# Units of gelu and gates: their loads move from SyncE's DMA queue to ScalarE's

## The reference, cut to what matters

```python
def peer(h, wq, k1, k2, u, v):
    ...
    experts = e1 * N_KEYS + e2
    gates = jax.nn.softmax(best, axis=-1).astype(h.dtype)
    ...
    def one_block(args):
        xb, eb, gb = args
        a = jnp.einsum("td,thkd->thk", xb, u[eb])
        act = gb * jax.nn.gelu(a)
        return jnp.einsum("thk,thkd->td", act, v[eb])
```

## Time and profile before

| | |
|---|---|
| median of 3 runs | 3135.79 us (3130.93 to 3138.95) |
| the profiled execution | 3137.47 us |
| its span, first to last instruction | 3135.7 us |
| TensorE busy | 2998.2 us (96%) |
| VectorE busy | 2533.5 us (81%) |
| ScalarE busy | 1030.0 us (33%) |
| GpSimd busy | 839.7 us (27%) |
| moved by DMA | 893.82 MB, mean 285 GB/s |
| queue q1 (SP) | 111376 packets, 491.29 MB |
| queue q0 (POOL) | 46080 packets, 335.56 MB |
| queue q10 (ACT) | 24624 packets, 64.45 MB |

### The profile page before, as it was taken

The page is one execution under the profiler, slowest core; times in us unless marked ns, Lnnn a source line. Parts: engine busy times, 40 slices in busy tenths (PEclk is TensorE's granted clock), DMA queues, the critical chain, the costliest instruction groups (busy, mean ns, idle before and its releaser), DMA issues.

```text
span 3135.7 us, 41987 instructions
## 1 busy us (share of the span) xinstructions
PE 2998.2 (96%) x17373; PEld 2759.4 (88%) x17373; DVE 2533.5 (81%) x3098; ACT 1030.0 (33%) x1081; POOL 839.7 (27%) x380
## 2 busy tenths in 40 slices
PE   5799989989989999999999999989999999999999
PEld 3687765557778899999999999989999999999999
DVE  7986968756673589999988998854989899898985
ACT  4323243341122333333333333323333334333331
POOL 5600000000030013333123333421444444444440
PEclk8999989989999999999999999999999999999999
DMA  9722223347744468888778988987999999999994
GB/s 368 268 94 77 81 85 138 124 168 302 290 159 180 142 228 326 333 333 321 274 266 343 356 346 337 389 330 285 375 395 389 390 392 392 395 386 398 385 399 164
DMA packets 182257, 893.82 MB, mean 285 GB/s; under 512 B 15680, under 2 KB 77248, under 8 KB 85824
## 3 DMA queue, kind: packets, MB, share of 16 engines
q1 hardware_dynamic: 111376, 491.29, 42.4%
q0 software_dynamic: 46080, 335.56, 26.2%
q10 hardware_dynamic: 24624, 64.45, 5.3%
HBM read 836.71 MB, written 54.53 MB: 284 GB/s over the span
## 4 chain that ended last, share of the span: by engine, by line
PE 84%; DVE 10%; DMA 2%; ACT 2%; issue 1%; SPq 0%; ACTq 0%; DVEq 0%; PEldq 0%
PE bank L1909 10%; PE bank L1911 10%; PE bank L1910 10%; PE bank L1968 10%; PE bank L1969 10%; PE bank L1970 10%; PE bank L1606 3%; PE bank L1608 3%; PE bank L1607 3%; DVE ada_w L944 2%; PE bank L1944 2%; PE bank L1843 2%; PE bank L1844 2%; PE bank L1845 2%; DMA ada_w<-wada 1%
## 5 line engine op out<-in xcount | busy, mean ns | idle before, releaser
L475 POOL DMA_INDIRECT u_row<-u_rows,urow_i x128 | 285.6, 2231 | 823.7 <-DVE u_row L1374 559.0
L1909 PE MATMUL bank<-act_hi,w_hi 128*128 128x352 f32 x1376 | 447.7, 325 | 8.0 <-DVE low L906 8.0
L1910 PE MATMUL bank<-act_lo,w_hi 128*128 128x352 f32 x1376 | 445.0, 323 | 0.0
L1968 PE MATMUL bank<-wt_hi,w_hi 128*128 128x352 f32 x1360 | 439.5, 323 | 4.9 <-DVE w_lo L906 4.4
L1969 PE MATMUL bank<-wt_lo,w_hi 128*128 128x352 f32 x1360 | 438.4, 322 | 0.0
L1911 PE MATMUL bank<-act_hi,low 128*128 128x352 f32 x1024 | 332.1, 324 | 0.0
L1911 PE MATMUL bank<-act_hi,w_lo 128*128 128x352 f32 x1024 | 330.3, 323 | 0.0
L1970 PE MATMUL bank<-wt_hi,w_lo 128*128 128x352 f32 x1024 | 330.3, 323 | 0.0
L1970 PE MATMUL bank<-wt_hi,low 128*128 128x352 f32 x1024 | 329.3, 322 | 0.0
L486 POOL DMA_INDIRECT u_row<-v_rows,urow_i x96 | 232.2, 2418 | 271.3 <-DVE y_g L1521 249.5
L1374 DVE SCALAR_TENSOR_TENSOR u_row<-u_row,h2t 128x2048 f32<-128x2048 f32 x128 | 288.9, 2288 | 13.4 <-DMA u_row<-u_rows,urow_i 13.3
(11 more groups left out here) (340 smaller groups left out, 7234.3 us busy)
## 6 DMA issues: line engine op xcount, KB each, us to landing
ada_w<-wada SPq DMA_DIRECT2D x80, 1024.0 KB, 5.5
w_raw<-u SPq DMA_DIRECT2D x64, 1024.0 KB, 5.9
raw<-u SPq DMA_DIRECT2D x64, 1024.0 KB, 5.6
w_raw<-v SPq DMA_DIRECT2D x64, 1024.0 KB, 9.1
raw<-v SPq DMA_DIRECT2D x64, 1024.0 KB, 6.8
w_raw<-win SPq DMA_DIRECT2D x27, 1024.0 KB, 4.9
gelu_scratch<-gelu_s ACTq DMA_DIRECT2D x128, 176.0 KB, 8.4
gate_scratch<-g_chunk ACTq DMA_DIRECT2D x11, 2048.0 KB, 12.2
```

The lines of the kernel that those rows point to most:

```text
L475: pool.indirect_dma_start(u_row[n % 3][:], None, urow_d, bass.IndirectOffsetOnAxis(ap=col, axis=0)).then_inc(u_row_loaded[n % 3], 16)
L1909: pe.matmul(out, wh[:, k, :], HD(k), start=(k == 0), stop=False)
L1910: pe.matmul(out, wh[:, k, :], LD(k), start=False, stop=False)
L1968: pe.matmul(o, wh[:, 8 * e + d, :], th, start=begin is not None and e == 0, stop=False)
```

## The change

`load_unit` leaves SP's program, whose queue then holds loads of weights alone, and goes into ScalarE's. SP also loses its waits for stored gelu and gates. Unit 0 is issued in `gelu_job`'s loop behind u = 115, unit 1 behind u = 120, unit 2 behind u = 125, unit 3 behind the `hi_raw` of v job 5, and unit 4 + 4i + r//4 behind the `hi_raw` of v job 6 + 16i + r where r % 4 == 2. Besides, `weigh_hi(0)` moves from u = 119 to 118, `weigh_hi(1)` from 124 to 123, and `weigh_lo(1)` from n = 126 to 125.

```diff
@@ SyncE
-            def load_unit(n):
-
-                if n:
-                    sp.wait_ge(wtl_ready, n)
-                rows = slice(4 * n, 4 * n + 4)
-                sp.dma_start(wt[:], gelu_d[:, rows, :]).then_inc(wt_loaded, 16)
-                sp.dma_start(gate_l[:], gate_d[:, :, rows, :].rearrange("c p i t -> p c i t")).then_inc(wt_loaded, 16)
-
-            for g in range(2, NKEY - 6):
+            for g in range(2, NKEY + 128):
                 load_raw(g)
-            for s in range(2):
-                sp.wait_ge(g_stored[s], DMA_LEAD + 16 * ((N_CH + 1 - s) // 2))
-                sp.wait_ge(gelu_stored[s], DMA_LEAD + 16 * 6)
-                sp.wait_ge(hot_used[2 * s + 1], LEAD + N_HOTS // 2)
-            load_unit(0)
...
-            load_unit(2)
-            for q in range(2, 128):
-                load_raw(NKEY + q)
-                if q == 2:
-                    for s in range(2):
-                        sp.wait_ge(gelu_stored[s], DMA_LEAD + 16 * NKEY // 2)
-                if q == 8:
-                    load_unit(3)
-                elif q % 4 == 2 and 10 <= q < 122:
-                    load_unit(4 + (q - 10) // 4)
@@ ScalarE
+            def load_unit(n):
+
+                if n:
+                    act.wait_ge(wtl_ready, n)
+                rows = slice(4 * n, 4 * n + 4)
+                act.dma_start(wt[:], gelu_d[:, rows, :]).then_inc(wt_loaded, 16)
+                act.dma_start(gate_l[:], gate_d[:, :, rows, :].rearrange("c p i t -> p c i t")).then_inc(wt_loaded, 16)
+
...
-                if u == 119:
+                if u == HOT + N_HOTS + 2:
+                    for s in range(2):
+                        act.wait_ge(g_stored[s], DMA_LEAD + 16 * ((N_CH + 1 - s) // 2))
+                        act.wait_ge(gelu_stored[s], DMA_LEAD + 16 * 6)
+                    load_unit(0)
+                if u == 118:
                     weigh_hi(0)
-                if u == 124:
+                if u == 120:
+                    load_unit(1)
+                if u == 123:
                     weigh_hi(1)
+                if u == 125:
+                    load_unit(2)
...
             for u in range(2):
                 act.wait_ge(gelu_stored[u], DMA_LEAD + 64 * 16)
+            load_unit(3)
...
                     if r % 4 == 0:
                         weigh_hi(3 + 4 * i + r // 4)
+                    if r % 4 == 2:
+                        load_unit(4 + 4 * i + r // 4)
@@ VectorE
-                elif n == 126:
+                elif n == 125:
                     weigh_lo(1)
```

More of the change, by code:

```diff
@@ L401, in _ @@
                 load_raw(u)
-            def load_unit(n):
-                if n:
-                    sp.wait_ge(wtl_ready, n)
-                rows = slice(4 * n, 4 * n + 4)
-                sp.dma_start(wt[:], gelu_d[:, rows, :]).then_inc(wt_loaded, 16)
-                sp.dma_start(gate_l[:], gate_d[:, :, rows, :].rearrange("c p i t -> p c i t")).then_inc(wt_loaded, 16)
-            for g in range(2, NKEY - 6):
-                load_raw(g)
-            for s in range(2):
-                sp.wait_ge(g_stored[s], DMA_LEAD + 16 * ((N_CH + 1 - s) // 2))
-                sp.wait_ge(gelu_stored[s], DMA_LEAD + 16 * 6)
-                sp.wait_ge(hot_used[2 * s + 1], LEAD + N_HOTS // 2)
-            load_unit(0)
[L418 to L422, removed]
-            load_unit(2)
-            for q in range(2, 128):
-                load_raw(NKEY + q)
-                if q == 2:
-                    for s in range(2):
-                        sp.wait_ge(gelu_stored[s], DMA_LEAD + 16 * NKEY // 2)
-                if q == 8:
-                    load_unit(3)
-                elif q % 4 == 2 and 10 <= q < 122:
-                    load_unit(4 + (q - 10) // 4)
+            for g in range(2, NKEY + 128):
+                load_raw(g)
         @block.gpsimd
```

## The result

The changed kernel takes **3168.51 us** (median of 4 runs, 3165.52 to 3169.83), against 3137.37 us for the kernel before in its 4 runs (3130.93 to 3142.16): ratio 1.0099, 95% interval 1.0079 to 1.0120, some 31 us **slower**. 3124 us were forecast. The time lies inside the range, on the side that the third rival (the gates starve, 3176 us, 30%) had named. The profiled execution took 3167.52 us; its span is 3165.7 us, 30.0 more than before. 893.82 MB are moved, as before; q10 (ACT) now carries 74800 packets, q1 (SP) 61200.

The account below looks back on a forecast made before the run. TensorE was taken as the bound, losing 24.9 us in three stalls behind late gates. Terms -2.0 - 13.9 + 3 + 1 = -11.9 turn the profiled 3137.5 into 3125.6; the runs' median is 1.7 lower: 3124 us, range 3107 to 3178.

Parts of the forecast that it names:

- third rival: Gates of units 4 to 31 starve at `weigh`, 2 us lost per unit on average: 3176 us, slower, chance 30%.
- What bounds the kernel: TensorE is full from 2250 to 3000 us; its idle time after 1400 us lies between 2050 and 2200 us.
- the three stalls: TensorE stalls while VectorE waits for gates of units 0, 1 and 3: 11.0, 6.8 and 7.1 us, together 24.9.
- The queue: Busy queues take turns packet by packet: 1408 gate packets need 2.4 us alone, 31 beside one queue, 56 beside two.
- ScalarE's own time: Two load issues a unit on ScalarE, at most 1.7 us each unit, claimed hidden: 0.
- SP: SP loses its unit issues and 16.6 us of waiting, so weights come sooner to a never idle TensorE: 0.
- Unit 0: Its 11.0 us stall: gates issued some 13 us sooner but landing near the old time; 2.0 us gained.
- a second way: Unit 0: gelu 116's store stands behind the unit's loads and `gelu_job(118)` waits for it, opening another way to the stall.
- Units 1 and 3: Their stalls of 6.8 and 7.1 us vanish through sooner issue: all 13.9 us gained.
- The steady units: Units 4 to 31: gates land later, settling at 17 to 20 us; 0.1 us per unit, 3 lost, bounds 0 to 140.
- the end: At the kernel's end VectorE, 3 us later, may hold TensorE by 0 to 3.5 us: 1 us lost.
- Landing does not care for the queue: Rival: units land as fast from issue as before and all three stalls go: 3111 us, chance 18%.

Follow-up runs that it names:

- e1: Changed kernel with all unit loads back on SyncE's queue, units 0 to 3 still issued sooner, units 4 to 31 at their old places: 3111.96 us.
- e4: Changed kernel with a unit's gates read in 128 packets of 5632 bytes instead of 1408 of 512 (correct gates left out): 3112.77 us.
- e7: Changed kernel with a unit's gates read in 512 packets of 1408 bytes instead of 1408 of 512 (correct gates left out): 3127.66 us.
- e5: Against e1, a unit's gelu load (128 long packets) moves to ScalarE's queue; its gates stay on SyncE's: 3111.99 us.
- e6: Against e5, the two loads change queues: gates (1408 small packets) on ScalarE's, gelu on SyncE's: 3210.38 us.
- e3: Kernel before with only units 4 to 31 loaded from ScalarE's queue as in the change, units 0 to 3 as before: 3161.22 us.
- e8: Against e1, gate table stored by unit, so loads get 5632-byte runs and the 11 stores on ScalarE's queue 512-byte ones: 3150.28 us.

## Why the prediction was wrong

**What held.** *What bounds the kernel* and the three stalls: e1 removes these three, adds 2 us at unit 4 and gains 23.3 us, against 24.9 read from the earlier trace rows. *The queue*: its turns go by packets and not by bytes. The prediction took this from equal counts in the earlier trace rows; e4 and e7 change only the number of packets, e5 and e6 only the queue of the small ones, and the times follow. Packets by queue in the changed kernel from 2194 to 2212 us, during unit 4's landing (packets, MB, share):

```profile
q0 software_dynamic: 671, 4.97, 67.0%
q1 hardware_dynamic: 299, 2.15, 28.9%
q10 hardware_dynamic: 629, 0.32, 6.2%
```

That is 629 packets of gates for 671 of POOL's rows, near one for one, at 35 per us, by which 1408 packets take 40 us. The Trainium skill, "DMA: Bandwidth & Descriptors", section "Queues, rings and completion order", has an engine drain some 9 to 17 descriptors of a ring per turn. The equal counts of the earlier trace rows, from which the prediction argued against such groups, can't decide that: groups of the same size in every queue give equal counts too. The end of unit 21's landing says more. From 2734 to 2748 us q10 moved between 1 and 7 packets in every single us while the queues of SP and POOL kept the DMA engines busy, so there they didn't travel in groups of 9 or more. *ScalarE's own time* for the issues of loads and *SP* at 0 held too: e5 has 32 of ScalarE's issues and none of the loss. What a store's issue costs behind a unit's gates (below) isn't in that term.

**Unit 0: 2.0 gained, was 7.3.** The landing was as named, issued at 2029.73 us and landed after 2055 (`weigh` at 2057.61), but TensorE lost 3.7 us and not 9, because VectorE stopped only 1.04 us in front of `weigh`. Of the 3.7, 2.0 fall at u job 119, for whose rest VectorE had to wait 6.15 us for a late `hi_raw`, and 1.7 at job 120, whose rest stands behind `weigh`. The prediction had named a second way, through `gelu_job(118)` and its store; the `hi_raw` was late by something else, the issue of that store, which took 12.15 us (below).

**Units 1 and 3: all 13.9 gained, was 5.0.** Unit 3 gave its 7.1. Unit 1 did not: its gates were issued at 2072.19, 21 us sooner than 2093.50, but took 30.55 us to land instead of 15.48. They landed 6 us sooner, while TensorE, spared 7.3 us at unit 0, needed them 7 us sooner. The step that failed is the sentence "Unit 1 has 15 us more, against 13.05 that were missing": it took the old landing time on the new queue. The paragraph on the queue, just above it, had given 31 us beside one busy queue and 56 beside two, and was applied to unit 0 and the steady units, not here.

**The steady units: 3 lost, were 39, and the end 1, was 2.7.** This term decided the sign: with it at 39, and the others as forecast, the sum is 24 us lost. Its mechanism stood in the prediction, and its bounds (0 to 140) held the truth; the value did not. "I expect it to settle at that edge", with landings of 17 to 20 us in every unit and 0.1 us lost, is the step that failed. Nothing settles: the 24 landings from 2250 to 3000 us have a median of 12.2 us, and five units of 28 come 2 to 13 us late for TensorE. The mean, 39 / 28 = 1.4 us, is nearer to the third rival's 2 and far above the 0.57 from which that rival decides. The prediction's own test, "Landings of 12 us there would mean that I misread the turn-taking", was a poor one, since a median says nothing of a few starved units; the other test, TensorE below 98%, was met (725.17 of 750 us, 96.7%).

**Landing does not care for the queue.** The time of this rival, 3111 us, is what the sooner issue gives on SP's queue (e1, 3111.96). The Trainium skill, same page, section "Issuing engines are not separate DMA queues", says that a second issuing engine saves only issue time. The runs differ: e5 and e6, which exchange only the queues of two loads, lie 98 us apart. That all transfers interleave on the same DMA engines, as it says, agrees with the counts above; but 629 packets of gates are 0.32 MB and 671 of POOL's 4.97, so they don't share them in proportion to their bytes.

**The rest.** Of the 31 us lost, by the terms: units 0 and 3 gained 7.3 + 7.1, unit 1 lost 2.1 more, the steady units 39, the end 2.7; that is 29.4, beside 30.0 between the spans.

## What to carry to other kernels

Count a transfer's packets before you move it onto another queue. Here, with the DMA engines full, a unit's 1408 small packets cost nothing that shows in line with the weights (e1, e5), and 26 to 98 us in all on ScalarE's queue (e3, e6), where they took turns with the large packets of the other queues; 128 long ones cost nothing that shows there either (e4, e5). And where a load comes late, try first to issue it sooner on the queue that it has.

## What the runs showed of the hardware that was not expected

**An issue can block its engine.** ScalarE's timeline in the changed kernel, behind the loads of unit 0:

```profile
2029.73 0.82 ACTq L807 DMA_DIRECT2D gate_l<-gate_scratch  x1
2035.16 0.46 ACT L782 ACTIVATE gelu_s<-bank 128x352 f32<-128x352 f32 x1 [4.01 <-PE bank L1903]
2035.66 12.15 ACTq L784 DMA_DIRECT2D gelu_scratch<-gelu_s  x1
2047.91 1.91 ACT L756 ACTIVATE hi_side<-raw 128x2048 fp32r<-128x2048 f32 x1 [12.28 <-issue]
```

The store's issue takes 12.15 us and keeps ScalarE from its next `hi_raw`, which has nothing to do with it. The issues of all 128 stores of the kernel before take at most 0.356 us; in e4 and e7, where a unit's gates are 128 and 512 packets, at most 0.342 and 0.343; in e8, behind stores in small packets, up to 18.144. So it shows only where the issuing engine's queue had been handed 1408 or more packets at once. Where it begins, between 512 and 1408, and whether their number is the cause wasn't measured.

**The last few packets can take most of a landing.** Unit 21's gates were issued at 2721.10. The queues in two short stretches of the changed kernel, 2728 to 2729 us, then 2740 to 2748:

```profile
q10 hardware_dynamic: 578, 0.30, 102.1%
q0 software_dynamic: 6, 0.04, 9.8%
```

```profile
q0 software_dynamic: 324, 2.40, 72.3%
q1 hardware_dynamic: 119, 0.93, 27.7%
...
q10 hardware_dynamic: 17, 0.01, 0.4%
```

In one us with the other queues nearly empty 578 of the 1408 packets passed; yet the unit landed only at 2751, with 17 packets in the 8 us before 2748. The trace doesn't tell the DMA engines apart, but the numbers suggest that a single one had gates left. The 16 engines moved 324 + 119 large packets in these 8 us, 3.5 per us each, and 2.1 packets of gates per us is about what one engine would move in turn with them (an estimate). A unit would then land quickly if an empty stretch lets every engine finish, and slowly if one engine misses it. That would explain why most landings lie near 11 us and a few reach 24 to 35, and why e6's runs differ by 44 us, but it is argued from these stretches and no run tested it.
